# RWKV head pairs on one core: other PSUM banks for the bonus and the turned operands, and the first direction's exponentials moved up into a buffer of their own

## The reference: what is computed

```python
r, k, v = xr @ w_r, xk @ w_k, xv @ w_v
kk = heads(k * k_k); kk = kk / jnp.maximum(jnp.sqrt(jnp.sum(kk * kk, -1, keepdims=True)), 1e-12)
for direction in range(2):
    w_log = -jax.nn.softplus(-(w0[direction] + jnp.tanh(xw @ w1[direction]) @ w2[direction])) - 0.5
    decay = jnp.exp(-jnp.exp(heads(w_log)))
    a = jax.nn.sigmoid(a0[direction] + (xa @ a1[direction]) @ a2[direction])
    k_d = heads(k * (1.0 + (a - 1.0) * k_a))
    y = y + wkv7_scan(r_h, decay, k_d, v_h, -kk, kk * a_h, reverse=(direction == 1))
    bonus = bonus + jnp.sum(r_h * k_d * r_k, -1, keepdims=True) * v_h
```

## Time and profile before

| what | us |
|---|---|
| median of 3 runs | 2227.78 |
| lowest and highest of them | 2227.05, 2231.99 |
| the profiled execution, device time | 2235.93 |
| its span, first to last instruction | 2234.2 |
| the 8 pairs in it | from 129 to 723 |
| one pair, bonus product to bonus product | 75.84 to 78.12 |

### The profile page before, as it was taken

The page is one execution under the profiler, slowest core; times in us unless marked ns, Lnnn a source line. Parts: engine busy times, 40 slices in busy tenths (PEclk is TensorE's granted clock), DMA queues, the critical chain, the costliest instruction groups (busy, mean ns, idle before and its releaser), DMA issues.

```text
span 2234.2 us, 46998 instructions
## 1 busy us (share of the span) xinstructions
PE 1975.7 (88%) x20190; PEld 1103.0 (49%) x20190; DVE 862.1 (39%) x1696; ACT 509.9 (23%) x988; POOL 191.1 (9%) x214
## 2 busy tenths in 40 slices
PE   3689999999998766999999977899996699999998
PEld 2257666766667343444444424566654344444442
DVE  6556565655554124222122211566632422112221
ACT  1133443444343010001111012355521000111100
POOL 0021133113302000000000000111100000000000
PEclk8899999999999877999999998899997799999999
DMA  2111011101100903999999961200050399999996
GB/s 79 32 33 35 9 38 35 40 8 35 39 10 9 381 0 134 429 429 427 429 429 428 428 278 40 106 20 20 20 237 0 137 429 428 428 429 429 428 428 283
DMA packets 78800, 450.00 MB, mean 201 GB/s; under 512 B 12733, under 2 KB 47162, under 8 KB 54074
## 3 DMA queue, kind: packets, MB, share of 16 engines
q1 hardware_dynamic: 78650, 447.73, 48.8%
HBM read 443.78 MB, written 3.93 MB: 200 GB/s over the span
## 4 chain that ended last, share of the span: by engine, by line
PE 68%; DMA 12%; DVE 6%; issue 6%; ACT 3%; DVEq 2%; ACTq 1%; POOLq 1%; SPq 0%; POOL 0%; PEldq 0%; another core or an unknown queue 0%
PE banks L1395 17%; DMA arena<-in_moe_w_down 11%; PE bank L597 7%; PE banks L1380 5%; PE banks L764 4%; PE banks L1246 4%; PE bank L1441 3%; PE bank L1395 3%; PE banks L868 2%; PE banks L1441 2%; PE banks L1783 2%; PE banks L454 1%; PE banks L951 1%; PE banks L1656 1%; PE banks L888 1%
## 5 line engine op out<-in xcount | busy, mean ns | idle before, releaser
L1395 PE MATMUL banks<-arena 128*64 128x512 f32 x2560 | 559.9, 594 | 1.1 <-ACT arena L1447 1.1
L1395 PEld LDWEIGHTS banks<-arena 128*64 128x64 f32 x2560 | 180.0, 137 | 355.2 <-issue 355.2
L597 PE MATMUL bank<-arena 128*128 128x512 f32 x384 | 192.1, 628 | 9.1 <-ACT arena L637 8.4
L1492 DVE TENSOR_TENSOR arena<-arena,bank 128x512 f32<-128x512 f32 x80 | 55.0, 687 | 367.3 <-PE bank L1441 367.3
L1099 POOL TENSOR_TENSOR arena<-arena 128x512 f32<-128x512 f32 x80 | 101.5, 1292 | 438.5 <-DVE arena L1154 438.5
L764 PE MATMUL banks<-arena 64*64 64x64 f32 x5632 | 126.3, 221 | 9.9 <-issue 6.4
L764 PEld LDWEIGHTS banks<-arena 64*64 64x64 f32 x5632 | 110.5, 134 | 48.4 <-issue 39.2
L1380 PE MATMUL banks<-arena 128*128 128x128 f32 x1024 | 123.5, 283 | 9.6 <-DVEq L347 9.6
L1380 PEld LDWEIGHTS banks<-arena 128*128 128x128 f32 x1024 | 120.4, 198 | 21.2 <-issue 11.4
L1395 PE MATMUL bank<-arena 128*64 128x512 f32 x512 | 115.5, 595 | 12.7 <-DMA arena<-in_moe_w_down 12.6
L1453 ACT ACTIVATE arena<-banks 128x512 f32<-128x512 f32 x32 | 19.1, 597 | 417.6 <-PE banks L1395 417.6
(11 more groups left out here) (297 smaller groups left out, 2617.9 us busy)
## 6 DMA issues: line engine op xcount, KB each, us to landing
arena<-in_moe_w_gate SPq DMA_DIRECT2D x64, 2048.0 KB, 21.7
arena<-in_moe_w_up SPq DMA_DIRECT2D x64, 2048.0 KB, 15.7
arena<-in_moe_w_down SPq DMA_DIRECT2D x64, 2048.0 KB, 16.5
arena<-in_x SPq DMA_DIRECT2D x8, 512.0 KB, 11.6
arena<-in_rw_wr SPq DMA_DIRECT2D x8, 512.0 KB, 3.9
arena<-in_rw_wk SPq DMA_DIRECT2D x8, 512.0 KB, 5.9
arena<-in_rw_wv SPq DMA_DIRECT2D x8, 512.0 KB, 6.0
arena<-in_rw_wo SPq DMA_DIRECT2D x1, 4096.0 KB, 18.0
```

The source lines that it names most:

```text
L597: last = nc.tensor.matmul(b[:, :], w_sl[:, n, k, :], xmix[n][:, k, :], start=(k == 0), stop=(k == ND - 1))
L1395: last = nc.tensor.matmul(ps[bank][z * CAP:(z + 1) * CAP, :], st[:, k, :], ring[c % RING][:, k, z * 512:(z + 1) * 512], start=(c % 2 == 0 ...
L1492: nc.vector.tensor_tensor(xs, xs, ps[b][:, :], ALU.add).then_inc(free[b], 1)
```

## The change

Three edits.

1. In the job order, the bonus and `vt` go to banks 0 and 1 and `at0`, `bt0` to banks 6 and 7; then `kt0` and `at1` to 0 and 1, `bt1` and `kt1` to 6 and 7. Before the first X, PE waits for the reading of `at1` (now the last in bank 1) instead of `kt1`.
2. `e_neg` gets a buffer of its own (512 more elements in each partition), and the wait for `kn` before the exponentials goes.
3. ACT's piece `cum` of direction 0 moves from level 1, after the square root, to level 0, ahead of the piece `k`. The order on DVE, PE, POOL and SP stays as it is.

```diff
-        e_neg = kraw
+        e_neg = body(S)
...
-            order += [(("bonus", u), 6), (("vt", u), 7), (("at0", u), 0), (("bt0", u), 1)]
+            order += [(("bonus", u), 0), (("vt", u), 1), (("at0", u), 6), (("bt0", u), 7)]
             order += [(("MR", 0, h, u), 2 + h) for h in range(2)]
-            order += [(("kt0", u), 6), (("at1", u), 7), (("bt1", u), 0), (("kt1", u), 1)]
+            order += [(("kt0", u), 0), (("at1", u), 1), (("bt1", u), 6), (("kt1", u), 7)]
...
                 act.wait_ge(cum_ready, 2 * u + piece[1] + 1)
-                if piece[1] == 0:
-
-                    job_full(act, jb, ("kn", u))
                 nc.scalar.activation(e_neg, cs, ACT.Exp, scale=-1.0)
...
-                job_read(pe, rj, ("kt1", u))
+                job_read(pe, rj, ("at1", u))
...
                     if lv == 0 and more:
+                        prep_act(act, ("cum", 0), rj, u)
                         prep_act(act, ("k",), rj, u)
                     if lv == 1 and more:
                         prep_act(act, ("kkn",), rj, u)
-                        prep_act(act, ("cum", 0), rj, u)
                         prep_act(act, ("r",), rj, u)
```

## The result

The changed kernel takes 2234.57 us (median of 20 runs, 2230.81 to 2241.91), the kernel before 2229.99 us (20 runs on the same chips, 2222.07 to 2236.36; it had shown 2227.78 in 3). The ratio is 1.0025, 95% interval 1.0014 to 1.0035: +5.6 us, between +3.1 and +7.8. I had forecast -1.5 us and at most +3.7. The profiled execution of the changed kernel happens to be short (span 2232.1 against 2234.2), so I don't compare spans: behind the pairs it takes 1506.5 us with PE's granted clock at 0.50, the lower of its two levels (1.2 GHz), in 170 of them, where the kernel before has 1511.4 us and 187 at the lower level. A second profile of the changed kernel has 1511.4 and 187 as well, so this difference is not the change's. The pairs, from the first bonus product to the last product of pair 7, took 590.4 us before and 595.7 after.

The account below looks back on a forecast made before the run. PE was taken to bound the kernel, busy 88% of the span. With the bonus's -1.3 us, the terms gave 0.0 to -3.0; the middle, -1.5, gave 2226.3 us on the median, range 2222.5 to 2231.5.

Parts of the forecast that it names:

- Banks: At the bonus product, its wait for DVE's reading of L goes: -1.3 us; moved transposes wait for nothing new.
- The exponentials at level 0: On ACT behind the last U copy, the three exponentials (1.8 us) fit into 4.72 us idle, cost nothing, need no load.
- The copy of r and x0: Before level 3, x0 starts 1.27 us sooner in pair 1, leaving PE some 1.15 ahead; 8.5 us over 7 pairs.
- DVE is late next: At T of level 3, PE waits for L1179's first instruction; in pair 1 only 0.23 of 1.15 us survive.
- A: Start of L1179 at level 3, fixed by DVE's chain; the forecast counted from here to v0, T following 0.79 us later.
- The load in front of the tanh: At level 3 the table load returns before w1's tanh, so v0 starts 2.65 us after the last U copy starts.
- Rival A: The table load falls where ACT is idle and costs nothing: -7.8 us with the bonus, 2220.0 us; chance 0.12.
- rival B: The table switch before the tanh costs more than its row: 9.0 or 9.7 us, 2235.3 or 2236.0; chance 0.06.
- The pauses: PE's pauses between T and last U copy, 3.1 us in all: staying gives +1.3 us, vanishing -1.7, before the bonus.
- rival C: Every pair has pair 4's 0.90 us pause between T and the copy: +3.3 us with the bonus, 2231.1; chance 0.10.
- Pair 7: The pair outside the waits view's stretch; its bonus wait, of the same size as the others, was left out.
- The clock: Other PE pauses or another clock in the later stages, outside the pairs, moving the time by over 4.5 us: chance 0.05.

Follow-up runs that it names:

- the three shifted profiles of the changed kernel: Unused small products added on PE ahead of the pairs of the changed kernel: 32 (ratio 1.0055), 32 in idle time (1.0022), 64 (1.0012), against the kernel before.
- the bank edit alone: Only the three lines of edit 1 put on the kernel before: 2227.22 us, ratio 0.9996.
- the exponentials alone: Edits 2 and 3 put on the kernel before, with its old banks: 2234.48 us, ratio 1.0026.
- with the early load: The changed kernel plus a one-column exponential on ACT right behind the square root, so the table load stands there: 2226.26 us, ratio 0.9990.
- with the shorter chain: The changed kernel plus the one-column exponential behind the root, DVE's reciprocal replaced by a constant multiplication (timing only): 2219.10 us, ratio 0.9941.

## Why the prediction was wrong, by its own steps

*Banks: right.* The wait of the bonus is gone; 0.27 us a pair, -1.9 over pairs 0 to 6, where I had -1.3. Pair 7 gave 0.3 back.

*The exponentials at level 0: right.* They ended at 224.44, ACT then idled 2.97 us, and no load stands there.

*The copy of r and x0: right.* x0 came 1.09 us sooner from the bonus (34.57 to 33.48), I had 1.15 to 1.27.

*DVE is late next: right.* T started 0.84 us after A in nearly every pair, I had 0.79. One part was too hopeful: I let A move forward by 0.66 us in pair 6 and by 0.12 in pair 2, where DVE had idled; in the sum A did not come sooner at all (+0.4).

*The load in front of the tanh: right.* v0 started 2.64 us after the U copy in all 7 pairs, forecast 2.65. Rival A is refuted by the row of the load, and rival B too: the switch costs 1.28 us and no more. The Trainium skill, "ScalarE: Activation LUTs", section "What ACT_TABLE_LOAD costs", has a drain of about 1.38 us beside it; here the load started 0.01 us after the copy's end (252.16 + 0.59 = 252.75, to 252.76), and by that page's figure v0 would have come at about +4.02, an estimate (2.64 + 1.38).

*The pauses: the step that failed.* I wrote: "If they vanish, because PE now stands still just before them and what feeds it can catch up: 45.5", let them stay at worst, and took the middle, 1.6 us. The pauses between T and the U copy, 3.1 us in my sum, became 4.6 and 3.8 us (26.0 and 25.2 less 7 x 3.06), and 4.5, 3.7 and 4.3 us in the three shifted profiles of the changed kernel. They did not vanish in any of the five. The runs put this in its place: a pause is a wait for a block of instructions, and its end is tied to the start of that block's fetch, not to how long PE stood still before. In pairs 0, 4 and 5 the fetch even starts later from T when PE had to wait for DVE at T. From the start rows of PE and the fetches' records (us; two profiles where there are two):

```
                                   fetch after T          pause behind it
pair 4  before                     0.38  0.64             0.67  0.93
        the bank edit alone        0.62                   0.87
        the exponentials alone     0.99                   1.54
        the changed kernel         0.98  0.97             1.27  1.27
        with the early load        0.97                   1.27
        with the shorter chain     0.06                   0.60
pair 0  before                     0.43  0.50             0.53  0.55
        the bank edit alone        0.79                   0.80
        the exponentials alone     1.55                   1.60
        the changed kernel         1.02  1.01             1.32  1.05
        with the early load        1.01                   1.05
        with the shorter chain    -0.33                   none
pair 5  before                     0.12  0.10             none  none
        the bank edit alone        0.22                   none
        the exponentials alone     0.75                   0.45
        the changed kernel         1.60  1.02             1.10  0.55
        with the early load        0.79                   0.32
        with the shorter chain     0.10                   none
```

The later the fetch, the longer the pause, and the kernel with the shorter chain, whose T waits for nothing, has both short. The wait at T is not all: with the bank edit alone the fetch of pair 0 comes 0.79 us after a T that waits for nothing. I had reckoned that PE's standing still at T would let its feeding catch up; in these pairs it is the wait at T, which the change made, that goes with the later fetch. That a fetch is not asked for while the queue stands at a waiting instruction would explain it, but is only argued. It is no general law either: in pair 2 the change made the pauses shorter (0.94 and 1.21 us at product 1006 before, 0.38 and 0.65 after), and with the instructions shifted by half a block T to the U copy takes 25.5 us in the kernel before and 25.9 and 25.2 in the changed one. So it is shown that the pauses don't vanish; that they grow is shown for three pairs and at one place in memory. My rival C, with +3.3 us, had the direction, but only for this stretch.

*Pair 7: the other failed step.* I counted the bank edit there and nothing else. It got 2.4 us longer in the first profile and 1.9 in the second. The bank edit accounts for 0.3: T at level 0 waits 1.83 us for DVE where it waited 1.54. In the first profile the fall of the granted clock to 0.50 adds 1.56 (the 128 products at 4.57 us instead of 3.01), and the pauses 0.5 (3.1 us in the pair, 2.6 before). In the second the clock stays at 1.00, and the pauses add 1.6 (4.2 us). So one term that I had at nothing is the clock, the other the pauses outside the stretch that I had cut out. That the pauses are a matter of where the blocks end is borne out by the kernel before with shifted instructions, whose pair 7 is 2.0 us longer with no other change.

*The clock: a term that I had at nothing.* I had allowed for another clock only in the later stages. Over the 13 profiles the clock falls inside the pairs 8 times, each for 3.41 us. Seven of these begin during or up to 1.2 us after the end of the longest waits: three at v0's wait for the tanh (1.73 to 1.76 us), four at the wait of T at level 0 of pair 7 (1.81 to 1.83 us). The eighth comes 1.9 us behind a pause of 1.62 us. The four profiles in which the exponentials stand at their old place (the kernel before, twice, shifted, and with the bank edit alone) have none; of the nine others, five have one or two. The waits that the change made are thus where the clock falls, in some executions and not in others. That they are the cause is likely but not shown, for the bank edit alone has the wait of 1.83 us and no fall.

*The sum.* From A to v0 I had 47.1 (the middle of 48.6 and 45.5); it took 50.4 and 49.6 us, against 46.5 and 46.1 in the kernel before. That is +3.7 on the mean of two profiles each. A came 0.4 later in the sum, which takes with it the 0.78 that I had hoped for in pairs 2 and 6; the rest of a pair gave -2.0, where I had -1.3 for the bonus; pair 7 adds +2.2, where I had 0. Together 3.7 + 0.4 - 2.0 + 2.2 = 4.3, but for rounding the +4.2 of the table, in place of -1.5. By terms, the 5.7 us between the two are: pauses from T to the copy +2.6 (4.2 on the mean, where I had 1.6), T after A +0.3, A itself +1.2, the rest of a pair -0.7, pair 7 +2.2, but for 0.1; the load and the tanh come out as forecast. The runs' +5.6 (3.1 to 7.8) agrees with +4.2; what lies between them can't be told from the spread of the later stages, which took 1506.5 us in one profile of the changed kernel and 1511.4 in the other. Banks, exponentials, x0, DVE's chain and the load were as forecast; but the forecast was a small difference of large terms, so the terms taken too low, the pauses and pair 7 above all, decided it.

## What to carry to other kernels

Where two functions on ACT need different tables, the question is not only how many loads there are but who waits behind each: moving the work that follows a load moves the load to the next function that needs it, and one tiny instruction of the right table pins it in idle time. When a wait is removed, look at the next engine's chain first (here DVE's, with no idle time left in front of it). Do not count on short pauses marked issue to vanish when the engine waits elsewhere, nor take them as constant: in dense stretches of small products they depend on where a block of instructions ends, and adding a few instructions far ahead moves them. And where one run of products takes longer with no gap in it, read the granted clock of that very window before looking for another cause.

## What the runs showed of the hardware

PE's instructions arrive in blocks of 16384 bytes: 110 fetches in the 8 pairs for 27395 products and weight loads, 249 of these to a block. In the densest stretches one fetch follows another after 3.3 us at the least, and PE stands up to 1.7 us until 2.1 to 3.3 us after the fetch began. The Trainium skill, "Runtime: NRT & Kernel Launch", section "Instruction fetch mechanics", has the blocks and calls the cost of crossing one mostly hidden, because instructions are issued more slowly than the blocks come; the blocks agree with the trace, the hiding does not for stretches of 64 x 64 products, of which L764 of the kernel before alone has 5632. The new thing for me was a third link, seen in pairs 0, 4 and 5 at one place in memory: where PE waits for another engine just ahead of a block's edge, the pause at that edge is longer (0.67 and 0.93 us against 1.27 in pair 4).

The granted clock can fall in the middle of a busy stage: from 1.00 to 0.50, 1.2 GHz, for 3.41 us, at a wait of 1.7 to 1.8 us in an engine that is busy for 73.90 of the 76.57 us of pair 1. At the two places in the changed kernel's first profile it cost 1.4 and 1.6 us, and it shows as slower products and not as a gap.
